# U pass of a PEER block: activations' high and low halves side by side, one 512-column matmul in place of two of 256 columns

## The chip, the cores and the metric

One core of one Trainium2 chip. The metric is the device time of the kernel in microseconds (us); lower is better. A profile of one execution lies beside the times.

## The reference, cut to what matters

The kernel computes one hybrid block: a mixer (pooling heads and latent attention), and then a feed-forward part, PEER, a retrieval over 16,384 single-neuron experts. Only the latter is touched:

```
def peer_ffn(h, w_q, sub_keys, expert_u, expert_v):       # h: 256 tokens x 2048
    q = (hf @ w_q).reshape(t, 8, 2, 128)
    sc = einsum('thpd,hpnd->thpn', q, sub_keys)           # scores against 2 x 128 sub-keys
    sv, si = top_k(sc, 16)                                # per head and half
    cand = sv[:, :, 0, :, None] + sv[:, :, 1, None, :]    # 16 x 16 pairs
    best, pos = top_k(cand, 16)
    eidx = ...                                            # 8 x 16 experts a token
    gate = softmax(best)
    u = take(expert_u, eidx);  a = einsum('ted,td->te', u, x)
    act = gelu(a, approximate=False) * gate
    vv = take(expert_v, eidx); out = einsum('te,ted->td', act, vv)
```

Everything is float32.

## The kernel before

The kernel gathers nothing: it multiplies all 16,384 experts with all 256 tokens, and puts the gates of the experts that were not picked to zero. So after the mixer there are three stages:

- The **U pass**: `acts = gelu(expert_u @ h2)`, in 128 tiles of 128 experts. A tile's 128x2048 floats of `expert_u` come as two halves of 128x1024 (512 KB each, four DMAs), into one of four buffers `raw`.
- The **gates** ("hot" stage): one-hot products spread the picked gates over the experts, and DVE multiplies them into `acts`.
- The **V pass**: `acts @ expert_v`, again in 128 tiles.

To keep float32's precision at the speed of the rounded type `fp32r`, each operand x is split in a high part xH (x rounded to `fp32r`) and a low part xL = x - xH, and each product is three: H·H, H·L and L·H. In the U pass the expert half is the stationary operand (`eH`, `eL`, three ring slots each), and the activations `h2H` and `h2L` (16 k-tiles of 256 tokens) are the moving one. The three products of a k-tile are `split3` (lines 603 to 605), all into one accumulation of 256 columns in one of the three PSUM banks `ps[:, 0..2, 0:256]`.

A half tile j goes through the engines so:

1. DMA (queue of SP) into `raw[j % 4]`, after the low part of half j-4 was made.
2. DVE transposes it in place in 32x32 blocks (`u_round`, line 1593).
3. ACT rounds it to `eH` (`u_high`, line 1151), once PE is through with half j-3, whose ring slot it takes (`u_used`).
4. The low part: DVE makes `eL` for even halves (`u_low`, line 1584), POOL for odd ones (`low_round`, line 504). Both subtract `eH` from `raw`.
5. PE: 8 k-tiles of 3 matmuls (`u_tile`).
6. After a tile's second half ACT applies Gelu straight from PSUM to `acts` (`gelu`, line 1164), and increments `a_out`. PE starts a tile once `a_out` says that the tile three before it has left its bank.

Each engine runs its own instructions in the order of the program; the kernel is written by hand in rounds of 6 tiles (12 halves), 21 rounds and 2 tiles more, of which most are hardware loops. DVE has other work in the U pass, placed between the transposes: for 16 groups of 6 halves (rounds 0 to 7) the top-16 of the sub-key scores, for 8 groups (rounds 8 to 11) the top-16 of the pairs, and in rounds 12 to 15 twelve steps that turn the picks into expert indices (`sub_keys`). One group's picks are six steps, one behind each half's transpose (and behind `u_low` where j is odd):

```
step 0: two copies cand<-sc  (pairs: two additions cand<-s16,s16)
step 1: two MAX8              step 2: two FIND_INDEX8, two MATCH_REPLACE8
step 3: two MAX8              step 4: two FIND_INDEX8
step 5: four small copies (CAST i16f/posu<-picked_at, COPY s/best<-picked)
```

Step 0 stands behind the first half of a group, step 5 behind the sixth.

## Time and profile before

| | before |
|---|---|
| device time, median of 3 runs | 2263.73 us (2262.08 to 2267.1) |
| profiled execution, span from first to last instruction | 2260.1 us |
| PE / DVE / ACT / POOL busy | 89% / 69% / 41% / 30% |
| U pass on PE, first to last matmul | 679.98 to 1421.28 us |
| V pass on PE | from about 1550 us to near the end |

The page names no device time of its own for the profiled execution; its span lies 3.6 us under the median of the runs, which also take in what stands ahead of the first and behind the last instruction. Times within a span are microseconds from its start. PE's busy time counts pipelined matmuls from their start to their modelled end; how fast it goes is read from the distance between starts. A line of the profile is that of the kernel before.

### The profile page before, as it was taken

Reading aid. Unit: us, or ns where it says so; the run is one execution under the profiler, and the core shown is the slowest. Engines: PE = TensorE matmul, PEld = TensorE weight load, DVE = VectorE, ACT = ScalarE, POOL = GpSimd, SP = SyncE. Lnnn points to the kernel's source line nnn. Section 1 sums busy time; section 2 is a strip of 40 time slices with the busy share of each in tenths; the row PEclk is TensorE's granted clock in tenths of the full one; section 3 lists DMA queues with packets and bytes.
Section 4 is the critical chain, followed back from the end, with each engine's and each line's share of the span. In section 5 each row is a group of like instructions: output and inputs, shape, how many; then the busy total and the mean of one; then the engine's idle time right before and its main releaser. Section 6 shows DMA issues by size and latency. Waiting matters only on the chain.

```text
span 2260.1 us, 38640 instructions
## 1 busy us (share of the span) xinstructions
PE 2012.3 (89%) x12649; PEld 1780.7 (79%) x12649; DVE 1555.6 (69%) x2214; ACT 918.7 (41%) x1399; POOL 687.8 (30%) x462
## 2 busy tenths in 40 slices
PE   1797978856889999999999999668999999999996
PEld 1675646745779999999999999657888888888885
DVE  5778679537449999999997666896555555555554
ACT  1133223335334444444444444564444444444443
POOL 0056015745644444444444444781000000000000
PEclk9988956888989999999999999999999999999998
DMA  9975586772956666666666666006565556555563
GB/s 355 359 276 218 201 325 236 274 192 76 274 155 179 185 182 180 182 181 184 176 176 183 182 182 170 28 0 218 192 193 193 193 191 193 193 194 192 193 194 121
DMA packets 264038, 439.13 MB, mean 194 GB/s; under 512 B 22242, under 2 KB 156688, under 8 KB 262192
## 3 DMA queue, kind: packets, MB, share of 16 engines
q1 hardware_dynamic: 262368, 427.89, 61.7%
q0 software_dynamic: 1600, 10.51, 1.2%
q8 instruction: 33, 0.54, 0.1%
q14 instruction: 21, 0.17, 0.0%
q10 hardware_dynamic: 16, 0.02, 0.0%
HBM read 434.12 MB, written 4.21 MB: 194 GB/s over the span
## 4 chain that ended last, share of the span: by engine, by line
PE 66%; DVE 19%; DMA 8%; issue 2%; ACT 2%; DVEq 1%; SPq 1%; POOL 0%; ACTq 0%; POOLq 0%
PE ps L926 10%; PE ps L923 10%; PE ps L924 10%; PE ps L603 10%; PE ps L605 10%; PE ps L604 10%; DMA ring<-in_ada_w_dram 7%; DVE acc L1272 6%; DVE acc_b L1272 6%; DVE hotB L1635 2%; PE ps L598 2%; DMA ring<-in_peer_wq_dram 1%; DVE acc_b L1269 1%; DVEq L1635 1%; PE ps L576 1%
## 5 line engine op out<-in xcount | busy, mean ns | idle before, releaser
L603 PE MATMUL ps<-h2H,eH 128*128 128x256 f32 x2048 | 580.1, 283 | 3.6 <-DVE eL L1584 2.3
L604 PE MATMUL ps<-h2L,eH 128*128 128x256 f32 x2048 | 579.6, 283 | 0.0
L605 PE MATMUL ps<-h2H,eL 128*128 128x256 f32 x2048 | 579.5, 283 | 0.0
L1666 DVE TENSOR_TENSOR eL<-raw,eH 128x1024 fp32r<-128x1024 f32 x256 | 313.5, 1225 | 338.3 <-ACT eH L1222 338.3
L504 POOL TENSOR_TENSOR eL<-raw,eH 128x1024 fp32r<-128x1024 f32 x128 | 311.0, 2430 | 451.7 <-ACT eH L1151 451.7
L1222 ACT CAST eH<-raw 128x1024 fp32r<-128x1024 f32 x256 | 269.9, 1055 | 385.4 <-PE ps L926 376.0
L923 PE MATMUL ps<-eH,aH 128*128 128x512 f32 x1024 | 399.0, 390 | 3.6 <-DVE eL L1666 3.6
L924 PE MATMUL ps<-eL,aH 128*128 128x512 f32 x1024 | 398.8, 389 | 0.0
L603 PEld LDWEIGHTS ps<-h2H,eH 128*128 128x128 f32 x2048 | 393.1, 192 | 4.6 <-POOL eL L504 1.7
L604 PEld LDWEIGHTS ps<-h2L,eH 128*128 128x128 f32 x2048 | 393.2, 192 | 0.0
L605 PEld LDWEIGHTS ps<-h2H,eL 128*128 128x128 f32 x2048 | 393.2, 192 | 0.0
L1593 DVE STREAM_TRANSPOSE raw<-raw 128x1024 f32<-128x1024 f32 x256 | 317.5, 1243 | 87.6 <-DMA raw<-in_peer_u_dram 79.3
L1151 ACT CAST eH<-raw 128x1024 fp32r<-128x1024 f32 x256 | 267.3, 1045 | 196.7 <-PE ps L605 158.7
L926 PE MATMUL ps<-eH,aL 128*128 128x512 f32 x1024 | 316.0, 390 | 0.0
L923 PEld LDWEIGHTS ps<-eH,aH 128*128 128x128 f32 x1024 | 192.6, 188 | 43.7 <-issue 3.7
L924 PEld LDWEIGHTS ps<-eL,aH 128*128 128x128 f32 x1024 | 192.6, 188 | 40.1
L926 PEld LDWEIGHTS ps<-eH,aL 128*128 128x128 f32 x1024 | 192.6, 188 | 40.0
L347 POOL TENSOR_TENSOR result<-x,scaled 128x2048 f32<-128x2048 f32 x1 | 4.5, 4471 | 712.1 <-DVEq L1687 712.1
L1584 DVE TENSOR_TENSOR eL<-raw,eH 128x1024 fp32r<-128x1024 f32 x128 | 154.1, 1204 | 32.9 <-ACT eH L1151 32.6
L1272 DVE SCALAR_TENSOR_TENSOR acc_b<-ring,c_act,acc_b 128x512 f32<-128x512 f32 x168 | 169.4, 1008 | 0.0
L1272 DVE SCALAR_TENSOR_TENSOR acc<-ring,c_act,acc 128x512 f32<-128x512 f32 x168 | 167.4, 996 | 0.6 <-DVE s_sb L1430 0.2
L1164 ACT ACTIVATE acts<-ps 128x256 f32 (+1 forms) x128 | 49.2, 385 | 224.6 <-PE ps L605 224.6
(267 smaller groups left out, 2717.6 us busy)
## 6 DMA issues: line engine op xcount, KB each, us to landing
raw<-in_peer_u_dram SPq DMA_DIRECT2D x1024, 128.0 KB, 2.9
raw<-in_peer_v_dram SPq DMA_DIRECT2D x256, 512.0 KB, 4.7
ring<-in_ada_w_dram SPq DMA_DIRECT2D x24, 4096.0 KB, 14.6
ring<-in_w_out_dram SPq DMA_DIRECT2D x4, 4096.0 KB, 20.0
ring<-in_peer_wq_dram SPq DMA_DIRECT2D x16, 1024.0 KB, 21.8
ring<-in_w_in_dram SPq DMA_DIRECT2D x3, 4096.0 KB, 13.5
ring<-in_w_uq_dram SPq DMA_DIRECT2D x1, 3072.0 KB, 18.1
ring<-in_w_in_dram SPq DMA_DIRECT2D x1, 2560.0 KB, 13.8
```

What stands on the lines that cost most here:

```text
L504: pool.tensor_tensor(by_k(eL[:, j % RING, :]), turned(raw[:, j % RAW, :]), by_k(eH[:, j % RING, :].bitcast(F32)), ALU.subtract).then_inc(u ...
L603: pe.matmul(o, lh, rh, start=start, stop=False, skip_group_check=True)
L604: pe.matmul(o, lh, rl, start=False, stop=False, skip_group_check=True)
L605: return pe.matmul(o, ll, rh, start=False, stop=stop, skip_group_check=True)
L923: pe.matmul(o[n], lh, vh[n], start=start, stop=False, skip_group_check=True)
L924: pe.matmul(o[n], lh, vl[n], start=False, stop=False, skip_group_check=True)
L926: mm = pe.matmul(o[n], ll, vh[n], start=False, stop=stop, skip_group_check=True)
L1151: act.copy(by_k(eH[:, j % RING, :]), turned(raw[:, j % RAW, :])).then_inc(u_hi, 1)
L1222: act.copy(eH[:, slot, :], raw[:, slot, :]).then_inc(v_hi, 1)
L1272: ins = dve.scalar_tensor_tensor(s_, w[:, k, :], c_act[:, k:k + 1], init[:, n % 2, :] if k == 0 else s_, ALU.mult, ALU.add)
L1593: dve.transpose(raw[:, j % RAW, :], raw[:, j % RAW, :]).then_inc(u_tr, 1)
L1666: dve.tensor_tensor(eL[:, slot, :], raw[:, slot, :], eH[:, slot, :].bitcast(F32), ALU.subtract).then_inc(v_lo, 1)
```

## The change

`h2H` and `h2L` are no longer two tensors one behind the other but one, `h2`, of [k-tile, 2, 256]: a k-tile's high and low halves lie side by side. So the two matmuls with the stationary `eH` become one with 512 columns into a full PSUM bank: `eH·h2H` lands in columns 0 to 255, `eH·h2L` in columns 256 to 511. `eL·h2H` is added to the first half as before. Before the Gelu the two halves of the bank must be added: ACT copies the second half to `asum` in SBUF (`cross_half`), DVE adds the first one from PSUM (`halves_sum`), and ACT's Gelu reads `asum`. The Gelu comes one tile later in ACT's program than before, the copy stands behind even `u_high`s, the addition behind the odd halves' `u_low`; PE's wait for a free bank is now for the addition (`a_sum`). `asum` has two buffers of 256 columns, in place of a row buffer that is no longer in use by then.

```
-    h2H = at("h2H", M, [KT, T], F32R)
-    h2L = at("h2L", M + 4096, [KT, T], F32R)
+    h2 = at("h2", M, [KT, 2, T], F32R)
+    h2H, h2L = h2[:, :, 0, :], h2[:, :, 1, :]
+    asum = at("asum", S + 688, [2, T])
...
             def u_tile(r, i, first):
                 if not first:
-                    pe.wait_ge(a_out, tile - 2)
+                    pe.wait_ge(a_sum, tile - 2)
...
-                        mm = split3(ps[:, bank, 0:T], eH[:, slot, k * P:(k + 1) * P], eL[:, slot, k * P:(k + 1) * P],
-                                    h2H[:, kk, :], h2L[:, kk, :], kk == 0, kk == KT - 1)
+                        pe.matmul(ps[:, bank, :], eH[:, slot, k * P:(k + 1) * P], h2[:, kk].rearrange("p a t -> p (a t)"),
+                                  start=kk == 0, stop=False, skip_group_check=True)
+                        mm = pe.matmul(ps[:, bank, 0:T], eL[:, slot, k * P:(k + 1) * P], h2H[:, kk, :],
+                                       start=False, stop=kk == KT - 1, skip_group_check=True)
...
-            def gelu(tile, bank):
+            def cross_half(tile, bank, half, first=False):
                 act.wait_ge(u_used, tile * 2 + 2)
-                act.activation(acts[:, bass.ds(tile, 1), :], ps[:, bank, 0:T], ACT.Gelu).then_inc(a_out, 1)
+                if first:
+                    act.wait_ge(row_stored, 128)
+                else:
+                    act.wait_ge(a_out, tile - 1)
+                act.copy(asum[:, half, :], ps[:, bank, T:2 * T]).then_inc(a_cross, 1)
+
+            def gelu(tile, half):
+                act.wait_ge(a_sum, tile + 1)
+                act.activation(acts[:, bass.ds(tile, 1), :], asum[:, half, :], ACT.Gelu).then_inc(a_out, 1)
...
-                    if j % 2 == 1 and not (first and j == 1):
-                        gelu(r * ROUND + (j // 2 - 1), (j // 2 - 1) % 3)
+                    if j % 2 == 0 and not (first and j < 4):
+                        cross_half(r * ROUND + (j // 2 - 2), (j // 2 - 2) % 3, j // 2 % 2, first and j < 8)
+                    elif j % 2 and not (first and j < 7):
+                        gelu(r * ROUND + (j // 2 - 3), (j // 2 + 1) % 2)
...
+            def halves_sum(tile, bank, half):
+                dve.wait_ge(a_cross, tile + 1)
+                dve.tensor_tensor(asum[:, half, :], ps[:, bank, 0:T], asum[:, half, :], ALU.add).then_inc(a_sum, 1)
...
                     if j % 2:
                         u_low(r, j - 1, first and j - 1 < RING)
+                        if not (first and j < 5):
+                            halves_sum(r * ROUND + (j // 2 - 2), (j // 2 - 2) % 3, j // 2 % 2)
```

What this makes of DVE's program, at the end of a group of picks of the sub-key stage and the start of the next (the loop of rounds 1 to 7; L1593 or L1613 is the transpose, L1584 or L1600 is `u_low`). Before:

```order
L1593 STREAM_TRANSPOSE raw<-raw 128x1024
L1581 REGISTER_ALU
L1583 REGISTER_ALU
L1584 TENSOR_TENSOR eL<-raw,eH 128x1024
L1539 ISA
L1539 COPY i16f<-picked_at 128x16
L1540 REGISTER_ALU
L1540 COPY s_66<-picked 128x16
```

And now:

```order
L1613 STREAM_TRANSPOSE raw<-raw 128x1024
L1597 REGISTER_ALU
L1599 REGISTER_ALU
L1600 TENSOR_TENSOR eL<-raw,eH 128x1024
L1604 REGISTER_ALU
L1605 TENSOR_TENSOR asum<-ps,asum 128x256
L1555 ISA
L1555 COPY i16f<-picked_at 128x16
```

The addition (L1605) has come between `u_low` and step 5's copies, and stands so at every odd half.

PE's program at the start of the U pass (ahead of it the transposes of the sub-keys and their scores). Before:

```order
L842 MATMUL ps<-cst,ring_49 128x128 x16
L854 MATMUL ps<-keyT,qT 128x128 x32
L603 MATMUL ps<-h2H,eH 128x256
L604 MATMUL ps<-h2L,eH 128x256
L605 MATMUL ps<-h2H,eL 128x256
```

And now (`h_144` is the tensor h2):

```order
L842 MATMUL ps<-cst,ring_49 128x128 x16
L854 MATMUL ps<-keyT,qT 128x128 x32
L867 MATMUL ps<-h_144,eH 128x512
L869 MATMUL ps<-h_144,eL 128x256
L867 MATMUL ps<-h_144,eH 128x512
```

Two matmuls and two weight loads a k-tile where there were three of each, with 768 columns as before.

## Rows read from the trace of the kernel before

**Rows 1.** The page: busy time by engine, and the chain that ended last.

```profile
PE 2012.3 (89%) x12649; PEld 1780.7 (79%) x12649; DVE 1555.6 (69%) x2214; ACT 918.7 (41%) x1399; POOL 687.8 (30%) x462
...
PE 66%; DVE 19%; DMA 8%; issue 2%; ACT 2%; DVEq 1%; SPq 1%; POOL 0%; ACTq 0%; POOLq 0%
```

**Rows 2.** Timeline, PE in the U pass: start, duration, engine, line, operation.

```profile
1200.07 0.28 PE L603 MATMUL ps<-h2H,eH 128*128 128x256 f32 x1
1200.19 0.28 PE L604 MATMUL ps<-h2L,eH 128*128 128x256 f32 x1
...
1421.28 0.28 PE L605 MATMUL ps<-h2H,eL 128*128 128x256 f32 x1
```

**Rows 3.** Windows, V pass: stretch, length, busy PE, PEld, DVE, ACT, POOL, PEclk, DMA, GB/s.

```profile
2000.00:2200.00 200.00, 200.00 (x885) 165.58 (x884) 102.49 (x110) 88.61 (x111) 0.00 (x0) 1.00 0.59 193
```

**Rows 4.** Windows, four stretches of the U pass.

```profile
692.87:948.60 255.73, 255.73 (x2134) 255.73 (x2133) 234.97 (x465) 106.28 (x134) 105.38 (x44) 1.00 0.68 183
948.60:1087.20 138.60, 138.60 (x1158) 138.60 (x1157) 135.94 (x248) 57.67 (x73) 57.55 (x24) 1.00 0.64 182
1087.20:1202.94 115.74, 113.28 (x940) 112.67 (x939) 107.27 (x79) 55.66 (x66) 52.16 (x20) 1.00 0.66 175
1216.00:1416.00 200.00, 200.00 (x1669) 200.00 (x1668) 123.87 (x103) 82.76 (x106) 83.35 (x35) 1.00 0.67 176
```

**Rows 5.** Timeline, first group of sub-key picks, step 5 and the next transpose.

```profile
687.95 1.25 DVE L1593 STREAM_TRANSPOSE raw<-raw 128x1024 f32<-128x1024 f32 x1 [0.45 <-DVE picked_at L1537]
689.12 1.18 DVE L1584 TENSOR_TENSOR eL<-raw,eH 128x1024 fp32r<-128x1024 f32 x1
689.23 1.05 ACT L1151 CAST eH<-raw 128x1024 fp32r<-128x1024 f32 x1 [1.16 <-DVE raw L1593]
690.22 0.17 DVE L1539 CAST i16f<-picked_at 128x16 f32<-128x16 uint32 x1
690.36 2.44 POOL L504 TENSOR_TENSOR eL<-raw,eH 128x1024 fp32r<-128x1024 f32 x1 [2.60 <-ACT eH L1151]
690.45 2.38 DVE L1540 COPY s<-picked 128x16 f32<-128x16 f32 x1
692.87 1.25 DVE L1593 STREAM_TRANSPOSE raw<-raw 128x1024 f32<-128x1024 f32 x1
```

**Rows 6.** Timeline, end of the second group of sub-key picks.

```profile
704.04 1.25 DVE L1593 STREAM_TRANSPOSE raw<-raw 128x1024 f32<-128x1024 f32 x1
706.42 1.05 ACT L1151 CAST eH<-raw 128x1024 fp32r<-128x1024 f32 x1 [1.61 <-PE ps L605]
706.54 0.17 DVE L1540 COPY s<-picked 128x16 f32<-128x16 f32 x1
707.54 2.40 POOL L504 TENSOR_TENSOR eL<-raw,eH 128x1024 fp32r<-128x1024 f32 x1 [3.25 <-ACT eH L1151]
```

**Rows 7.** Timeline, one group of pair picks: first, last half.

```profile
1000.92 1.25 DVE L1593 STREAM_TRANSPOSE raw<-raw 128x1024 f32<-128x1024 f32 x1
1001.38 2.39 POOL L504 TENSOR_TENSOR eL<-raw,eH 128x1024 fp32r<-128x1024 f32 x1 [3.36 <-ACT eH L1151]
1002.09 2.31 DVE L1525 TENSOR_TENSOR cand<-s 128x256 f32 x2
1015.51 1.25 DVE L1593 STREAM_TRANSPOSE raw<-raw 128x1024 f32<-128x1024 f32 x1
1018.01 0.16 DVE L1540 COPY best<-picked 128x16 f32 x1
1018.31 1.25 DVE L1593 STREAM_TRANSPOSE raw<-raw 128x1024 f32<-128x1024 f32 x1
```

**Rows 8.** Timeline, gates stage: a DVE product with one operand in PSUM, and POOL.

```profile
1442.12 0.62 POOL L518 TENSOR_TENSOR hotP<-cst,slotT 128x256 f32<-128x256 f32 x1 [0.75 <-PE ps L901]
1442.18 0.67 DVE L1641 TENSOR_TENSOR acts<-acts,ps 128x512 f32 x1
```

**Rows 9.** Timeline, ACT's last Gelu.

```profile
1421.60 0.38 ACT L1164 ACTIVATE acts<-ps 128x256 f32<-128x256 f32 x1 [5.37 <-PE ps L605]
```

More of the change, by code:

```diff
@@ L260, in hybrid_block @@
         u_tr, u_hi, u_lo, u_lo_pool, u_used = sem("u_tr"), sem("u_hi"), sem("u_lo"), sem("u_lo_pool"), sem("u_used")
-        a_out = sem("a_out")
+        a_cross, a_sum, a_out = sem("a_cross"), sem("a_sum"), sem("a_out")
         hot_pool, hot_act, hot_abs, hot_diff = sem("hot_pool"), sem("hot_act"), sem("hot_abs"), sem("hot_diff")
@@ L1188, in _ @@
             u_round(ROUNDS, TILES % ROUND)
+            cross_half(TILES - 2, (TILES - 2) % 3, 0)
+            gelu(TILES - 3, 1)
+            cross_half(TILES - 1, (TILES - 1) % 3, 1)
+            gelu(TILES - 2, 0)
             gelu(TILES - 1, 1)
@@ L1627, in _ @@
             u_round(ROUNDS, TILES % ROUND)
+            halves_sum(TILES - 2, (TILES - 2) % 3, 0)
+            halves_sum(TILES - 1, (TILES - 1) % 3, 1)
             def hots(g, half, first):
```

## The prediction

> **What bounds the kernel now.** I read the page's busy times and its chain first [rows 1]: PE is busy for 89% and carries 66% of the chain, DVE 19%. That is an average, so next the stretches of the stage that is changed. In the U pass PE is 100% busy in the two stretches of picks and after them, at granted clock 1.00 [rows 4]; the timeline shows matmuls of 256 columns starting 0.12 us apart without a gap [rows 2]. Counted over the last stretch it is 200 us / 1669 = 0.1198 us [rows 4]. So a half tile takes 24 x 0.12 = 2.88 us on PE, a group of six halves 17.28, and PE sets the pace. But look at DVE in the same rows: 234.97 of 255.73 us (92%) while it picks sub-keys, 135.94 of 138.60 (98%) while it picks pairs, 107.27 of 115.74 (93%) with `sub_keys`, and only 62% after that. In three of the four stretches the second engine is full behind the first, and the change takes time from PE and gives work to DVE.
>
> **PE's part.** The V pass has matmuls of 512 columns, each with its own weight load: 200 us / 885 = 0.226 us apart, at the same clock [rows 3]. So columns cost 0.106 us per 256, and each pair of load and matmul about 0.013 us on top. A k-tile of the U pass goes from 3 x 0.12 = 0.36 us to 0.226 + 0.12 = 0.346, a tile from 5.76 to 5.536, a half to 2.768, a group to 16.6 us. Over 128 x 16 k-tiles that is 27.6 to 29 us, if PE stays the bound. The bounds of this price are nothing (a matmul of 512 costing two of 256) and this.
>
> The Trainium skill ("TensorE: Matmul & The Clock Gate", Back-to-back issue gap) gives N/2.4 + 2.5 ns for the distance of two matmuls at full clock: 109 and 216 ns, by which a k-tile would save 2.5 ns and the whole pass 5 us. The rows have 120 and 226, so I go by the rows.
>
> **DVE's part.** One addition a tile, 256 columns, one operand in PSUM. The nearest row is DVE's product of 512 columns with PSUM, 0.67 us [rows 8]; a DVE row of 1024 columns from SBUF is 1.18 [rows 5], next start 1.10 after its own, so about 1.04 ns a column. That leaves 0.67 - 0.27 = 0.40 for the addition, of which 0.34 keeps the next one waiting (a duration less 0.07 of overlap). Bounds: 0.27 (columns alone) and 0.45.
>
> Whether it can get stuck: in rows 8 POOL began a subtraction with two SBUF operands at 1442.12, and DVE's product began 0.06 later and still took 0.67, so an addition of this kind doesn't wait for POOL. The opposite kind is in rows 5 and 7. POOL's `eL` ran from 690.36 to 692.80; DVE's small copy of 690.45, otherwise 0.17 us, ended at 692.83. And the first of two pair additions, begun at 1002.09, waited for the end of POOL at 1003.77, after which both took 0.63. Copies in SBUF and additions with both operands there stand still until POOL is through.
>
> The Trainium skill says the same ("SBUF — State Buffer", Who interferes with whom): a DVE instruction with at most one SBUF input outside the two-port modes doesn't contend with GpSimd, two SBUF inputs or a two-port copy do. By that rule the new addition is safe and the old copies aren't.
>
> What matters is therefore not the 0.34 us alone but where step 5's copies now fall. Take T as the start of a group's sixth transpose. If ACT waits for nothing else, its rounding starts 1.28 later, and POOL's `eL` runs from T + 2.41 to T + 4.85 (687.95, 689.23, 690.36 and 2.44 long) [rows 5]. The four copies start at T + 2.27 now: three slipped in ahead of POOL there, and the fourth was caught. In the second group DVE had caught up, ACT waited for PE until 706.42, POOL began only at T + 3.50, and all four copies slipped by [rows 6]. So before, DVE loses its time to POOL in step 0 instead (1.68 us in rows 7), and still keeps up. With the addition the copies come to T + 2.60, behind POOL's start: all four stand until T + 4.85, and the next transpose starts at T + 5.16 rather than T + 2.6.
>
> **DVE's cycle after the change.** Sub-key group without any lock: 692.87 to the end of the last copy 706.71, 13.84 us [rows 5, 6]. Take out the last 2.6, put in 5.16, and two more additions of 0.34 (the third is inside the lock): 17.08. Step 0 then meets no POOL. Pair group: 1000.92 to 1018.31 is 17.39, less 1.68 of lock and 0.14 of waiting = 15.57 [rows 7]; less 2.66, plus 5.16, plus 0.68 = 18.75. Both are over PE's 16.6, so DVE becomes the bound, ACT waits for DVE and not for PE, and the assumption that POOL starts at T + 2.41 holds itself up: DVE never gets the lead that let the copies escape. It is a tight thing at the entry: in the second group T would come near 704.97, its transpose end at 706.2, and PE would be ready for ACT at 705.4, 0.8 us earlier.
>
> Sum, in PE's time, against the profiled 2260.1:
> - Sub-key stage, some 15 groups of 17.08 in place of 17.28: -3.
> - Pair stage, 8 groups of 18.75 in place of 17.28: +11.7.
> - The 38 halves with `sub_keys`. DVE's 115.7 us hold 8.5 of idleness [rows 4]; most of it goes (-6.5), 19 additions come (+6.4, of which some 1.3 inside locks), and the four big products behind odd halves, which begin at 2.27 after their transpose and now at 2.60, fall behind POOL's start as the copies do; I put that at 3 us over those locks that are there already: 117.3. PE took 38 x 2.88 = 109.4 for these halves, and 4 of gaps: the whole pass lasted from 679.98 to 1421.4 [rows 2], 4.1 more than 128 x 5.76, and of the four stretches this is the only one in which PE wasn't busy throughout [rows 4]. 117.3 in place of 113.4: +4.
> - The 74 halves left, DVE at 62%: 74 x 0.113 = -8.4.
> - The end: ACT's Gelu started right behind the last matmul [rows 2, 9]. Now a copy of 0.38, the addition 0.40 and two handovers of 0.1 stand ahead of it: +1.
>
> Together +5.3: span 2265.4. The median of the runs lies 3.6 above the profile's span, so 2269. Elsewhere nothing moves: ACT's copies (0.38 a tile) fall in an engine that is 42% busy in these stretches [rows 4], and PE's wait for `a_sum` is for an addition that stands in DVE's program ahead of the `eL` which the same tile needs anyway.
>
> **The rivals.**
> 1. *DVE keeps its lead (faster).* If at the entry, or after any pause of PE, POOL's `eL` starts past T + 2.9, the copies escape and the lock falls in step 0, at least 1.2 us. Then a sub-key group needs 13.84 + 1.02 + 1.2 = 16.1 and runs at PE's 16.6 (-10.9 over 16), the pair group at 15.57 + 1.02 + 1.2 = 17.8 (+4), `sub_keys` at +2, the rest as above: -12, so 2252. For it: the state of before is of this kind. Against: it takes 0.8 us that DVE doesn't have at the start. 0.16. It decides from the point where ACT waits for PE at the sixth half.
> 2. *The saving shows in full*, DVE's additions hidden: -27.6 + 1, 2237. Against it, 98% in rows 4. 0.05.
> 3. *The addition is dearer*, 0.45 us a piece or a wait for ACT's copy in DVE's queue, behind which everything stands: 0.1 more for two additions in each of 24 groups and half as many after, some +6: 2275. 0.12.
> 4. *A matmul of 512 saves nothing*: the stages bound by DVE stay, the last loses its -8.4: 2277. For it there is no row, against it rows 3. 0.06. The formula of the Trainium skill cited above ("TensorE: Matmul & The Clock Gate", Back-to-back issue gap) would come out here but for 2.5 ns a k-tile.
> 5. *The lock is half as long in the pair stage* (POOL held up by DVE's own `eL` now and then): +1, 2265. 0.09.
> 6. *The addition waits for POOL after all*: 2 us in most odd halves, +50 and more. Rows 8 speak against it. 0.02.
>
> The forecast itself has 0.50, with a range of its own from 2264 to 2274.
>
> **How the numbers follow.** A measurement of this kernel tells about 0.2% (4.5 us) from no change, so "same" is 2259.2 to 2268.3. The forecast's middle is just above that edge: 0.3 of its 0.5 is slower and 0.2 same. Slower: 0.3 + 0.12 + 0.06 + 0.02 = 0.50. Same: 0.2 + 0.09 + 0.02 (of rival 1) = 0.31. Faster: 0.14 + 0.05 = 0.19. The range takes in rivals 1, 3, 4 and 5 and leaves out 2 and 6: 2250 to 2279.
>
> **What would show it.** In the changed kernel's trace: matmuls 0.226 and 0.12 us apart in the last stretch, which then runs at 5.54 us a tile; PE idle in small gaps, some 0.5 us a group in the sub-key stage and 2 in the pair stage, waiting for `eL`; ACT's roundings there released by DVE's transposes, not by PE; the copies of step 5 at over 2 us and those of step 0 short; DVE near 100%. Wrong would be: step 0 still carrying the lock with ACT released by PE (rival 1), additions over 0.5 us (3 or 6), or spacing that doesn't add to 0.346 (4).

## The result, and the profile after

| | before | after |
|---|---|---|
| device time, median | 2263.38 us (2262.08 to 2267.1, 4 runs) | 2274.93 us (2273.46 to 2278.31, 4 runs) |
| span of the profiled execution | 2260.1 us | 2272.2 us |
| U pass, first to last matmul | 741.3 us | 747.6 us |

The ratio is 1.005, interval 1.0036 to 1.0064: the kernel became 11.5 us slower, where 5.3 were forecast; its median lies 5.9 over the forecast's 2269. One execution of the kernel before, beside the second set of experiments, took 2896 us at a granted clock of 0.65 and is left out of every comparison. The page of the changed kernel, busy time by engine, the chain that ended last, and two groups that the change touches ([rows 1] are the first two lines before; the last line here is the group of ACT's roundings in the kernel before):

```profile
PE 2002.0 (88%) x10601; PEld 1668.7 (73%) x10601; DVE 1598.0 (70%) x2342; ACT 955.6 (42%) x1527; POOL 686.0 (30%) x462
...
PE 50%; DVE 28%; DMA 10%; issue 6%; ACT 3%; SPq 2%; DVEq 1%; POOL 0%; ACTq 0%; POOLq 0%
...
L867 PE MATMUL ps<-h,eH 128*128 128x512 f32 x2048 | 723.1, 397 | 21.5 <-DVE eL L1600 21.2
...
L1153 ACT CAST eH<-raw 128x1024 fp32r<-128x1024 f32 x256 | 269.1, 1051 | 386.5 <-DVE raw L1613 279.2
...
L1151 ACT CAST eH<-raw 128x1024 fp32r<-128x1024 f32 x256 | 267.3, 1045 | 196.7 <-PE ps L605 158.7
```

PE has 2048 matmuls fewer, as it should, and in the chain PE gave way to DVE: 50% for 66%, 28% for 19%. PE's first matmul of a half now waits 21 us in all for DVE's low part, and most of ACT's idle time before its roundings, 279.2 of 386.5 us, ends with a transpose of DVE, where before 158.7 of 196.7 ended with PE. The stage by stage view is the windows of the U pass, cut at the same transposes as [rows 4] (length, busy time of PE, PEld, DVE, ACT and POOL, granted clock, DMA share, GB/s); the last one is 200 us out of the stretch behind them:

```profile
696.88:955.40 258.52, 256.42 (x1446) 220.46 (x1445) 252.11 (x510) 122.28 (x181) 107.96 (x45) 1.00 0.68 183
955.40:1106.28 150.88, 139.62 (x771) 117.53 (x770) 148.23 (x273) 64.43 (x96) 57.47 (x24) 1.00 0.60 167
1106.28:1221.45 115.17, 108.25 (x607) 92.34 (x606) 110.53 (x99) 59.99 (x84) 49.21 (x19) 1.00 0.65 173
1230.00:1430.00 200.00, 200.00 (x1155) 176.11 (x1154) 135.77 (x141) 95.50 (x144) 86.00 (x36) 1.00 0.72 183
```

Against [rows 4]: the sub-key stretch 258.5 us for 255.7, the pairs 150.9 for 138.6, the stretch with `sub_keys` 115.2 for 115.7. The granted clock is 1.00 in all. In the first two PE is no longer full (it has 0.14 and 1.4 us of idleness a group, where 0.5 and 2 were forecast) and DVE is, at 98% both times. From there to the last matmul it is 210.0 us for 218.3; counted over the last row, 1155 matmuls in 200 us are 0.346 us for each pair of them. So the whole account of the U pass is +0.1 before the first of these marks, +2.8, +12.3, -0.6, -8.3: +6.3.

In what follows a small copy or an addition is called caught, or in a lock, when it lasts until POOL's subtraction is through instead of its usual few tenths of a microsecond. The timeline of DVE, POOL and ACT in the second group of sub-key picks, around the sixth transpose (start, duration, engine, line, operation, and in brackets the idle time before and what ended it), which answers to [rows 5] and [rows 6]:

```profile
708.71 1.25 DVE L1613 STREAM_TRANSPOSE raw<-raw 128x1024 f32<-128x1024 f32 x1
709.99 1.05 ACT L1153 CAST eH<-raw 128x1024 fp32r<-128x1024 f32 x1 [0.46 <-DVE raw L1613]
710.99 0.41 DVE L1605 TENSOR_TENSOR asum<-ps,asum 128x256 f32<-128x256 f32 x1
711.12 2.40 POOL L504 TENSOR_TENSOR eL<-raw,eH 128x1024 fp32r<-128x1024 f32 x1 [2.49 <-ACT eH L1153]
711.32 2.24 DVE L1555 CAST i16f<-picked_at 128x16 f32<-128x16 uint32 x1
...
713.93 1.25 DVE L1613 STREAM_TRANSPOSE raw<-raw 128x1024 f32<-128x1024 f32 x1
```

Read it from T = 708.71. ACT is released by the transpose, not by PE as in [rows 6]. POOL starts at T + 2.41, the addition ends in time for the first small copy at T + 2.61, and that copy takes 2.24 us until POOL is through. The next transpose stands at T + 5.22. Step 0 behind it is quick: its two copies take 0.32. From the third group on one time is different: POOL starts later behind ACT's rounding.

```profile
727.07 1.25 DVE L1613 STREAM_TRANSPOSE raw<-raw 128x1024 f32<-128x1024 f32 x1 [0.95 <-DMA raw<-in_peer_u_dram]
728.35 1.05 ACT L1153 CAST eH<-raw 128x1024 fp32r<-128x1024 f32 x1 [1.39 <-DVE raw L1613]
729.56 2.39 POOL L504 TENSOR_TENSOR eL<-raw,eH 128x1024 fp32r<-128x1024 f32 x1 [3.81 <-ACT eH L1153]
```

Now T = 727.07, and POOL starts at T + 2.49. The first two groups are the round that is written out, the others run in hardware loops: in all 13 traces here POOL's subtraction starts 0.077 us behind the end of ACT's rounding in the six odd halves of the first round and the two of the last, and 0.157 in the loop between them. The next transpose stands 5.17 to 5.29 behind T there, but for the last group of pairs.

The groups of DVE's instructions over the picks, before and after, show where the lock has gone (line, operation, count, busy us, mean ns). Before, from 710 to 1080:

```profile
L1528 DVE COPY cand<-sc 128x128 f32 x28 | 32.7, 1207 | 0.0
L1525 DVE TENSOR_TENSOR cand<-s 128x256 f32 x16 | 18.6, 1199 | 0.0
L1539 DVE CAST i16f<-picked_at 128x16 uint32 x28 | 4.5, 168 | 0.0
```

After, from 710 to 1100:

```profile
L1555 DVE CAST i16f<-picked_at 128x16 uint32 (+1 forms) x30 | 36.8, 1232 | 0.0
L1605 DVE TENSOR_TENSOR asum<-ps,asum 128x256 f32<-128x256 f32 x66 | 27.3, 414 | 0.0
...
L1541 DVE TENSOR_TENSOR cand<-s 128x256 f32 x16 | 5.8, 399 | 0.0
L1544 DVE COPY cand<-sc 128x128 f32 x28 | 4.5, 201 | 0.0
```

Step 0's copies and additions fell from 1207 and 1199 ns to 201 and 399, and step 5's first copies rose from 168 to over 1200. They come in pairs of which one is caught and one is short, so the mean hides a piece of 2.2 or 2.3 us in each. The addition itself costs 27.3 us in 66 pieces and was never caught: over the pass it is 410 ns at least and 425 at most.

### The profile page after: what moved, and what is told of

Read it like the earlier page. It is cut to its first block, busy times and chain, and to the rows that moved or that the text cites. A ratio compares the mean times of both kernels' runs of the same rounds, so it can differ in the third digit from the quotient of the medians.

```text
span 2272.2 us, 35008 instructions
## 1 busy us (share of the span) xinstructions
PE 2002.0 (88%) x10601; PEld 1668.7 (73%) x10601; DVE 1598.0 (70%) x2342; ACT 955.6 (42%) x1527; POOL 686.0 (30%) x462
## 4 chain that ended last, share of the span: by engine, by line
PE 50%; DVE 28%; DMA 10%; issue 6%; ACT 3%; SPq 2%; DVEq 1%; POOL 0%; ACTq 0%; POOLq 0%
PE ps L925 10%; PE ps L926 10%; PE ps L928 10%; PE ps L867 10%; DVE acc L1288 6%; DMA ring<-in_ada_w_dram 6%; DVE acc_b L1288 5%; PE ps L869 5%; DVE raw L1613 2%; DVE eL L1600 2%; DVE hotB L1659 2%; PE ps L598 2%; DMA raw<-in_peer_u_dram 2%; ACT eH L1153 2%; DMA init<-in_ada_b_dram 1%
## 5 line engine op out<-in xcount | busy, mean ns | idle before, releaser
L867 PE MATMUL ps<-h,eH 128*128 128x512 f32 x2048 | 723.1, 397 | 21.5 <-DVE eL L1600 21.2
L869 PE MATMUL ps<-h,eL 128*128 128x256 f32 x2048 | 573.2, 280 | 0.0
L867 PEld LDWEIGHTS ps<-h,eH 128*128 128x128 f32 x2048 | 384.0, 188 | 122.8 <-DVE eL L1600 31.5
L1153 ACT CAST eH<-raw 128x1024 fp32r<-128x1024 f32 x256 | 269.1, 1051 | 386.5 <-DVE raw L1613 279.2
L869 PEld LDWEIGHTS ps<-h,eL 128*128 128x128 f32 x2048 | 386.5, 189 | 0.0
L1613 DVE STREAM_TRANSPOSE raw<-raw 128x1024 f32<-128x1024 f32 x256 | 316.8, 1241 | 78.7 <-DMA raw<-in_peer_u_dram 69.9
L1600 DVE TENSOR_TENSOR eL<-raw,eH 128x1024 fp32r<-128x1024 f32 x128 | 152.5, 1192 | 11.5 <-ACT eH L1153 11.1
L1288 DVE SCALAR_TENSOR_TENSOR acc<-ring,c_act,init 128x512 f32<-128x512 f32 x24 | 27.1, 1131 | 129.3 <-DMA ring<-in_ada_w_dram 111.9
L474 POOL TENSOR_TENSOR ring_low<-ring,win_high 128x512 fp32r<-128x512 f32 (+1 forms) x48 | 67.2, 1436 | 141.4 <-ACT win_high L991 141.2
L474 POOL TENSOR_TENSOR ring_low<-ring,wq_high 128x512 fp32r<-128x512 f32 x64 | 93.4, 1490 | 49.7 <-ACT wq_high L991 48.7
```

The costliest lines, as they stand in the source:

```text
L867: pe.matmul(ps[:, bank, :], eH[:, slot, k * P:(k + 1) * P], h2[:, kk].rearrange("p a t -> p (a t)"), start=kk == 0, stop=False, skip_group ...
L869: mm = pe.matmul(ps[:, bank, 0:T], eL[:, slot, k * P:(k + 1) * P], h2H[:, kk, :], start=False, stop=kk == KT - 1, skip_group_check=True)
L1153: act.copy(by_k(eH[:, j % RING, :]), turned(raw[:, j % RAW, :])).then_inc(u_hi, 1)
L1288: ins = dve.scalar_tensor_tensor(s_, w[:, k, :], c_act[:, k:k + 1], init[:, n % 2, :] if k == 0 else s_, ALU.mult, ALU.add)
L1600: dve.tensor_tensor(by_k(eL[:, j % RING, :]), turned(raw[:, j % RAW, :]), by_k(eH[:, j % RING, :].bitcast(F32)), ALU.subtract).then_inc(u_ ...
L1613: dve.transpose(raw[:, j % RAW, :], raw[:, j % RAW, :]).then_inc(u_tr, 1)
```

## The experiments

Two theories stood against each other at the start. The first: the additions fill DVE, and what decides is which of DVE's SBUF copies meet POOL's subtraction. The second: PE saves little by itself, and the additions or the waits cost what they cost wherever they stand. Medians are set beside runs of the kernel before on the same chip (2262.3, 2262.2 and 2262.4 us in the three sets). A "group" is six halves, timed from transpose to transpose in the one execution that was profiled. One number is the mean of a stage's groups, of which single ones lie some 0.6 us to either side. The first group of a stage is left out, and so are single ones in which DVE also waited for data: in the changed kernel the one of 18.31. First the table, then the edits.

| run | median, us | ratio and interval | sub-key group | pair group | last stretch, a group |
|---|---|---|---|---|---|
| after | 2274.9 | 1.005 (1.0036 to 1.0064) | 17.05 to 17.22 | 18.83 to 18.95 | 16.64 |
| copies early | 2252.05 | 0.9958 (0.9942 to 0.9975) | 16.64 | 17.31 | 16.96 |
| copies early, kernel before | 2262.96 | 1.0 (0.999 to 1.0009) | 17.28 | 17.28 | 17.28 |
| no addition | 2242.96 | 0.9915 (0.9898 to 0.9931) | 16.96 | 16.96 | 16.96 |
| addition twice | 2291.66 | 1.013 (1.0113 to 1.0147) | 17.75 to 17.88 | 19.49 to 19.61 | 16.64 |
| both moved | 2248.57 | 0.9935 (0.9918 to 0.9953) | 16.9 | 16.9 | 16.64 |
| addition behind the copies | 2254.72 | 0.9963 (0.9948 to 0.9978) | 15.6 to 16.96 | 17.32 | 16.96 |
| POOL adds | 2273.03 | 1.0053 (1.0033 to 1.0073) | 16.96 | 17.4 to 17.7 | 16.64 |
| addition within SBUF | 2279.96 | 1.0077 (1.0055 to 1.0099) | 17.18 to 17.37 | 18.9 to 19.0 | 16.64 |
| kernel before with additions | 2277.6 | 1.0062 (1.0042 to 1.0083) | 17.10 to 17.27, then 15.07 to 17.39 | 18.84 to 18.95 | 17.28 |
| spread | 2244.52 | 0.992 (0.9905 to 0.9935) | 16.64 | 16.64 | 16.64 |
| turned order | 2241.23 | 0.9899 (0.9884 to 0.9914) | 16.7 | 16.7 | 16.7 |

**Step 5's copies early.** The four copies stand directly behind the sixth transpose, ahead of `u_low`, when POOL can't have started:

```
                     dve.transpose(raw[:, j % RAW, :], raw[:, j % RAW, :]).then_inc(u_tr, 1)
+                    if pairs is not None and j % 6 == 5:
+                        pick_step(r * 2 + j // 6, 5, pairs)
                     if j % 2:
                         u_low(r, j - 1, first and j - 1 < RING)
...
-                    if pairs is not None and not (first and j == 0):
+                    if pairs is not None and not (first and j == 0) and j % 6 < 5:
                         pick_step(r * 2 + j // 6, j % 6, pairs)
```

> Changed kernel with the four copies of step 5 moved ahead of the even half's eL subtraction (they start 1.2 us after the sixth transpose's start, before POOL can begin at 2.4). Lock theory (DVE is the bound and loses 2.2 us a group behind POOL at step 5): a sub-key group falls from 17.16 us to PE's 16.6, a pair group from 18.9 to about 17.6 (what is left is some 1 us of lock at step 0); in all -8 and -10, so about 2256 us, 7 below the kernel before. Work theory (the additions' own 0.34 us are what costs, the lock only moves to step 0): a pair group stays over 18.5, the time within 3 us of 2275. Handover theory (ACT's copy and the longer chain to Gelu delay PE): no change, 2275.

2252.05 us, 10.3 below the kernel before where the changed one is 11.5 above it, so some 22 us better, with every addition still in place. The groups of DVE, 710 to 1080, of this run:

```profile
L1544 DVE COPY cand<-sc 128x128 f32 x26 | 27.6, 1100 | 0.0
...
L1541 DVE TENSOR_TENSOR cand<-s 128x256 f32 x16 | 12.8, 838 | 0.0
...
L1555 DVE CAST i16f<-picked_at 128x16 uint32 x28 | 4.0, 150 | 0.0
```

The lock is back in step 0, where it was before the change, and step 5 is short again. A lock there is cheaper, since step 0 comes when POOL has already run for a part of its 2.4 us, as in [rows 7]: against the 0.20 and 0.40 that these pieces take in the changed kernel it costs 1.8 us in a sub-key group, where PE sets the pace again, and 0.9 in a pair group, where step 5's cost 2.1. So some two thirds of what the additions seemed to cost (31 us, below) hung on the place of four copies of 0.17 us.

**The same edit in the kernel before.**

> The kernel before with the same move of step 5's copies, a control. Lock theory: PE is the bound there and DVE has no gain to pass on, 2263 within 3 us. Rival (the move helps by itself, since DVE lies on the path at the start and in the stretch with the index steps): 5 us or more below 2263.

2262.96 us, no change, groups 17.28: there PE sets the pace, and the place of the copies is worth nothing. The gain of the first run comes only where DVE is the bound.

**No addition.** ACT copies the first half of the bank to `asum`, and nothing is added; `eH·h2L` is left out of the result:

```
-                    pe.wait_ge(a_sum, tile - 2)
+                    pe.wait_ge(a_cross, tile - 2)
...
-                act.copy(asum[:, half, :], ps[:, bank, T:2 * T]).then_inc(a_cross, 1)
+                act.copy(asum[:, half, :], ps[:, bank, 0:T]).then_inc(a_cross, 1)
...
-                act.wait_ge(a_sum, tile + 1)
+                act.wait_ge(a_cross, tile + 1)
...
-                            halves_sum(r * ROUND + (j // 2 - 2), (j // 2 - 2) % 3, j // 2 % 2)
```

> Changed kernel without DVE's addition: ACT's copy takes the first half of the bank instead of the second, and Gelu reads that, so the product eH x h2L is left out of the result; PE and ACT do all that they do in the changed kernel. Lock and work theory alike: DVE is back at 13.8 us a sub-key group and keeps its lead, PE sets 16.6 us there and about 17 in the pair stage, the last stretch 16.6; together about 2240 (2234 to 2246). Handover theory (ACT's copy in the chain, or matmuls of 512 in this mix, cost the time): 2265 to 2275.

2242.96 us: the matmuls and ACT's copies alone are worth 19.4 us against the kernel before, and the additions as the change places them cost 31 (19.4 and 11.5). That ACT's copy or the longer way to the Gelu should cost the time is out. Its profiled execution was the longest of the four, 2251.58 us; the last section comes back to it.

**The addition twice** (the first of the two into columns of the bank that nobody reads any more):

```
                 dve.wait_ge(a_cross, tile + 1)
+                dve.tensor_tensor(ps[:, bank, T:2 * T], ps[:, bank, 0:T], asum[:, half, :], ALU.add)
                 dve.tensor_tensor(asum[:, half, :], ps[:, bank, 0:T], asum[:, half, :], ALU.add).then_inc(a_sum, 1)
```

> Changed kernel with each addition done twice (the first result goes to the bank's other half and is not used). If DVE is the bound: 0.34 us for each of the two additions of a group that stand outside the lock, 24 groups, +16, and some +5 in the stretch with the index steps, nothing after it: about 2296. If DVE were not the bound (handover theory): under +5, 2280.

2291.66 us. DVE's timeline at the sixth half of this kernel:

```profile
710.97 0.42 DVE L1605 TENSOR_TENSOR ps<-ps,asum 128x256 f32<-128x256 f32 x1
711.31 0.41 DVE L1606 TENSOR_TENSOR asum<-ps,asum 128x256 f32<-128x256 f32 x1
711.64 1.90 DVE L1555 CAST i16f<-picked_at 128x16 f32<-128x16 uint32 x1
...
713.91 1.25 DVE L1614 STREAM_TRANSPOSE raw<-raw 128x1024 f32<-128x1024 f32 x1
```

The second addition starts 0.34 us after the first; the caught copy is shorter by as much (1.90 for 2.24), and the next transpose stands at 713.91 as it stood at 713.93. An addition inside the lock costs nothing, the two others of a group 0.34 each: the groups grew by some 0.65. That is the price that the prediction gave it.

**Both moved.** As the first, and step 0 too goes ahead of POOL's start: behind the second transpose of a group instead of the first, ahead of `u_low`:

```
...
+                    if pairs is not None and j % 6 == 1 and not (first and j == 1):
+                        pick_step(r * 2 + j // 6, 0, pairs)
                     if j % 2:
                         u_low(r, j - 1, first and j - 1 < RING)
+                        if pairs is not None and j % 6 == 1 and not (first and j == 1):
+                            pick_wait(r * 2 + j // 6, 1)
...
```

> Changed kernel with step 5's copies ahead of the even half's eL, as in the run before, and step 0's two operations moved behind the next half's transpose, ahead of its eL, where POOL has ended. Lock theory: no copy or pick addition waits for POOL any more; a pair group falls from 17.3 us to 16.65 (15.57 + 1.02 of additions, as much as PE's 16.6), a sub-key group stays at PE's pace; 8 x 0.65 = 5 us less than with the copies alone, about 2247. Rival (17.3 us a pair group is plain DVE work and not a lock at step 0): within 2 us of 2252.

2248.57 us, 13.6 below the kernel before where the copies alone gave 10.3. DVE's groups, 710 to 1080:

```profile
L1613 DVE STREAM_TRANSPOSE raw<-raw 128x1024 f32<-128x1024 f32 x131 | 162.9, 1244 | 37.0 <-DMA raw<-in_peer_u_dram 32.4
...
L1541 DVE TENSOR_TENSOR cand<-s 128x256 f32 x16 | 5.7, 399 | 0.0
```

Step 0 is free of POOL as step 5 is, and DVE has 37 us to spare ahead of its transposes where it now waits for data; PE is the bound in the pair stage again.

**The addition behind the copies**, in the sixth half alone. The prediction would have it that the copies then start at T + 2.27, where three slip by and the fourth is caught, as in [rows 5]:

```
-                        if not (first and j < 5):
+                        if not (first and j < 5) and not (pairs is not None and j % 6 == 5):
...
                         pick_step(r * 2 + j // 6, j % 6, pairs)
+                    if pairs is not None and j % 6 == 5:
+                        halves_sum(r * ROUND + (j // 2 - 2), (j // 2 - 2) % 3, j // 2 % 2)
```

> Changed kernel with the addition of the sixth half behind step 5's copies instead of ahead of them, nothing else moved. Place theory (what hurts is that the addition pushes the copies behind POOL's start): three copies slip by, all is well, below 2263. Lock theory in full (with DVE as the bound POOL starts 2.41 us after the transpose and the fourth copy is caught at 2.5, as in the first group of the kernel before; one caught copy costs as much as four): 17.1 us a sub-key group, 18.9 a pair group, 2275 to 2278.

2254.72 us, 20 below the 2275 to 2278 that were expected. The timeline in the second group and in a pair group:

```profile
710.12 2.44 POOL L504 TENSOR_TENSOR eL<-raw,eH 128x1024 fp32r<-128x1024 f32 x1 [2.50 <-ACT eH L1153]
710.21 2.38 DVE L1556 COPY s<-picked 128x16 f32<-128x16 f32 x1
...
999.26 2.45 POOL L504 TENSOR_TENSOR eL<-raw,eH 128x1024 fp32r<-128x1024 f32 x1 [3.13 <-ACT eH L1153]
999.27 0.17 DVE L1556 COPY best<-picked 128x16 f32 x1
```

The fourth copy was caught in the first two groups, 2.38 us. From the third on ACT's rounding still begins at T + 1.28 where DVE releases it, but POOL starts at T + 2.49 in place of T + 2.41, with the later handover of the loop, and the copy (999.27, with POOL in front at 999.26) gets through in 0.17. The groups shrink to 15.6 to 16.5 us while DVE catches up, and then ACT waits for PE in the sub-key stage. The escape doesn't need that: in the pair stage ACT is released by DVE's transpose again, at T + 1.28, and the copies get through in all eight groups. What the expectation had wrong was POOL's start, read from [rows 5], the first group, outside the loop. The same few tenths of DVE's work, on the other side of four short copies, are worth 20 us.

**POOL adds.** ACT copies the whole bank of 512 columns, POOL adds its halves behind its own `eL`, with the copies early; PE's wait for a bank is then for ACT's copy:

```
+            def halves_sum(tile):
+                pool.wait_ge(a_cross, tile + 1)
+                pool.tensor_tensor(asum[:, 0, :], asum[:, 0, :], asum[:, 1, :], ALU.add).then_inc(a_sum, 1)
...
-                    act.wait_ge(a_out, tile - 1)
-                act.copy(asum[:, half, :], ps[:, bank, T:2 * T]).then_inc(a_cross, 1)
+                    act.wait_ge(a_out, tile)
+                act.copy(asum[:].rearrange("p a t -> p (a t)"), ps[:, bank, :]).then_inc(a_cross, 1)
```

> Copies of step 5 early as in the first run; ACT copies the whole bank (512 columns) to SBUF and POOL adds the halves there (behind its own eL) in place of DVE; Gelu and copy follow one another in ACT. DVE has 13.84 and 15.57 us of its own a group and at most 2 us of lock at step 0 behind a POOL that is now busy 0.6 us longer: 16.6 a sub-key group, 17.2 a pair group, less waiting in the stretch with the index steps; about 2246 (2240 to 2252). If POOL's addition delays its next eL or DVE's eL: 2255 and more.

2273.03 us, a miss by 27. The sub-key groups run at 16.96 as hoped, but with `sub_keys` a group takes 19.2 to 21.5 us. POOL's additions from 720 to 940, then from 1110 to 1220, and one of the latter with what DVE did:

```profile
L511 POOL TENSOR_TENSOR asum<-asum 128x256 f32<-128x256 f32 x39 | 29.0, 743 | 0.0
...
L511 POOL TENSOR_TENSOR asum<-asum 128x256 f32<-128x256 f32 x16 | 25.6, 1600 | 0.0
...
1140.10 2.10 DVE L1608 TENSOR_TENSOR eL<-raw,eH 128x1024 fp32r<-128x1024 f32 x1
1141.08 1.72 POOL L511 TENSOR_TENSOR asum<-asum 128x256 f32<-128x256 f32 x1
```

The same addition takes POOL 743 ns in one stage and 1600 in the other. Fourteen of the 16 in the second began while DVE's `u_low`, a subtraction with both operands in SBUF, was running, and took 1.71 to 1.74 us; the two others took 0.73. So POOL is held by DVE as DVE is by POOL, and the low part that PE waits for comes late: 12.0 us of PE's idleness in this stretch end with POOL's `eL`.

**The addition within SBUF.** ACT copies the whole bank as above, DVE adds the two SBUF halves at the place of the change:

```
-                dve.tensor_tensor(asum[:, half, :], ps[:, bank, 0:T], asum[:, half, :], ALU.add).then_inc(a_sum, 1)
+                dve.tensor_tensor(asum[:, 0, :], asum[:, 0, :], asum[:, 1, :], ALU.add).then_inc(a_sum, 1)
```

> Changed kernel, with ACT copying the whole bank (512 columns) to SBUF and DVE adding the two halves there: the same DVE work, but two operands in SBUF. If such an addition shares a port with POOL: it starts some 0.14 us ahead of POOL's eL, which then begins 0.25 later, and with it the end of the lock: 17.3 us a sub-key group, 19.1 a pair group, some +5, 2280; where POOL is first, the addition takes over 2 us. If it shares nothing: 17.16 and 18.9, 2275, and no addition over 0.45 us.

2279.96 us, where I had put it, and the timeline shows the hold that was under test, though shorter than expected. One of the first groups, and a sixth half in the loop:

```profile
705.71 0.41 DVE L1605 TENSOR_TENSOR asum<-asum 128x256 f32<-128x256 f32 x1
705.85 2.54 POOL L504 TENSOR_TENSOR eL<-raw,eH 128x1024 fp32r<-128x1024 f32 x1 [2.19 <-ACT eH L1153]
...
728.57 0.42 DVE L1605 TENSOR_TENSOR asum<-asum 128x256 f32<-128x256 f32 x1
728.78 2.44 POOL L504 TENSOR_TENSOR eL<-raw,eH 128x1024 fp32r<-128x1024 f32 x1 [3.19 <-ACT eH L1153]
728.90 2.36 DVE L1555 CAST i16f<-picked_at 128x16 uint32 x1
```

The addition begins up to 0.2 us before POOL's subtraction and is through undisturbed, the copy behind it is caught. But now POOL is held: in the two stages of picks its subtraction takes 2.53 to 2.54 us where 0.28 us of the addition were left at its start, 2.44 to 2.48 where some 0.2 were left (35 times), and 2.38 to 2.41 where less was left or nothing. In the changed kernel, whose addition has one operand in PSUM, the same overlaps leave it at 2.38 to 2.42. The other direction was met once: the addition at 1431.19, which began when 0.19 us of POOL's subtraction were left, took 0.47 us, the longest of the 128. The groups are 0.07 to 0.08 us longer, which isn't all of the 6 us between the two kernels, and the rest wasn't looked for.

**The kernel before, with additions.** The three matmuls of 256 columns stay. ACT's copies and DVE's additional instructions stand as in the change; as there is no second half to add, DVE takes the maximum of the bank and its copy, which leaves the values as they are:

```
...
+                act.copy(asum[:, half, :], ps[:, bank, 0:T]).then_inc(a_cross, 1)
...
+                dve.tensor_tensor(asum[:, half, :], ps[:, bank, 0:T], asum[:, half, :], ALU.max).then_inc(a_sum, 1)
```

> Only the DVE and ACT half of the change, without PE's: three matmuls of 256 columns as before, all into the first half of the bank; ACT copies that half to asum, DVE takes the maximum of PSUM and asum (equal numbers, so the result stays) with the same shapes as the addition, Gelu from asum. If DVE's cycle is what costs: sub-key groups 17.2 to 17.3 (DVE's 17.16 just below PE's 17.28), pair groups 18.9 in place of 17.28, +13, the stretch with the index steps +2 or 3, the rest at 17.28: about 2278 (2274 to 2282), slower than the changed kernel by what PE gains there in the last stretch. If the matmuls of 512 columns had a part in the loss: about 2265.

2277.6 us. Windows of the pair stage and of the stretch behind the picks, and what ACT waited for from 968 to 1100 (us in all, times, longest):

```profile
968.00:1100.00 132.00, 125.15 (x1018) 122.51 (x1017) 129.61 (x239) 56.34 (x84) 50.13 (x22) 1.00 0.58 166
1240.00:1420.00 180.00, 180.00 (x1503) 180.00 (x1502) 123.39 (x126) 84.77 (x128) 74.60 (x32) 1.00 0.71 182
```

```profile
ACT eH L1151 <- DVE raw L1611: 75.9, 42, 4.0
```

DVE's side alone, with ACT released by its transposes, makes the pair groups 18.9 us long, the same as in the changed kernel, whatever PE's matmuls cost. With DVE loaded so, the wide matmul is worth some 4 us (15.2 above the kernel before without it, 11.5 with it); without the additions it was worth 19.4. The last stretch, where DVE has room, keeps 17.28 a group here for 16.64. In the sub-key stage DVE's 17.2 us are just below PE's 17.28: in eleven groups a copy of step 5 is caught, from the twelfth on ACT waits for PE long enough for all to get through, until the pair stage.

**Spread.** Both moved, and the twelve steps of `sub_keys` no longer behind halves 4, 7, 10 to 37 but further apart:

```
-                    at_ = j + 2 * ROUND * i - 4
-                    if at_ >= 0 and at_ % 3 == 0 and at_ // 3 < 12:
-                        sub_keys(at_ // 3)
+                    places = (4, 8, 11, 14, 18, 21, 24, 28, 31, 34, 38, 41)
+                    if j + 2 * ROUND * i in places:
+                        sub_keys(places.index(j + 2 * ROUND * i))
```

> Both picks' steps moved as in e5, and the twelve index steps at halves 4, 8, 11, 14, 18, 21, ... in place of every third: the big products with two SBUF operands behind even halves alone, where POOL is at most 1 us from its end, the sums (which take no second port) behind odd ones. Lock theory: the 38 to 42 halves of this stretch go from 117 us to near PE's pace (48 halves in 136 rather than 142), 2242 (2239 to 2246). Rival (the stretch is bound by DVE's plain work, 2.3 us a step): 2247 to 2250.

2244.52 us, as expected (2239 to 2246); the 38 halves with `sub_keys` take 109.7 us where both moved, the kernel that it is made from, needed 116.9 and the changed one 115.2.

**Turned order.** The last, and in every second k-tile the matmul with `eL` stands first, so that the sequence is 512, 256, 256, 512:

```
...
+                        if kk % 2:
+                            low()
+                            mm = high()
+                        else:
+                            high()
+                            mm = low()
```

> e10 with the order of the two matmuls turned in every second k-tile, so that two of 512 and two of 256 columns follow one another. In the traces so far PE goes at one of two paces when nothing holds it up, 0.3467 or 0.3533 us a k-tile, in the same program. If the alternation of 512 and 256 columns is what makes the slower pace possible: 0.346 throughout, some 10 us below e10, 2232. If not: the same two paces and e10's time within 3 us.

2241.23 us, all four executions within 2240.34 to 2242.51, where the five of the kernel it is made from lay between 2241.7 and 2248.56. The 2232 that were expected if the alternation alone made the slower pace did not come, and the 3.3 us under that kernel lie within the spread of its executions. It beats both kernels: 21 us or 1% under the one before, some 33 under the changed one. What the traces show of the order is told at the end.

## Why the prediction was right or wrong

The direction was called, with the mechanism; the size was half of what came: +5.3 forecast, +11.5 measured, +12.0 between the two profiled spans. By its steps:

- *PE's part.* 0.346 us a k-tile was forecast, and the last stretch has 0.346. The bound "a matmul of 512 columns saves nothing" (rival 4) is out: the saving is 13 ns a k-tile (17.28 less 16.64 us over 48). The formula of the Trainium skill ("TensorE: Matmul & The Clock Gate", Back-to-back issue gap), which that section gives for isolated matmuls, made it 2.5 ns, and the trace doesn't agree. One thing was not seen, that this pace has a second value, with half the saving (below).
- *DVE's part.* The addition was put at 0.40 with 0.34 on the path: 0.41 and 0.34. It was never held (425 ns at most), nor did DVE wait ahead of it in the picks, so rivals 3 and 6 are out. In the changed kernel only two of the 128 began while POOL was at work, but with the addition twice 90 did, and none of them took over 0.44 us. The rule of the Trainium skill ("SBUF — State Buffer", Who interferes with whom) that an instruction of DVE with at most one SBUF input, outside its two-port modes, doesn't contend with GpSimd agrees with these.
- *The lock moves from step 0 to step 5.* Forecast were copies at T + 2.60 and the next transpose at T + 5.16; measured 2.61 and 5.22, and in the loop 2.61 and 5.17 to 5.29, as POOL starts 0.08 us later there than in [rows 5]. The copies-early run and the one with the addition behind them show that this, more than DVE's load as such, is what costs: they give 22 and some 20 us back with all additions in place, of the 31 that the additions cost. The unchanged result of the same edit in the kernel before shows that it matters only where DVE is the bound.
- *DVE keeps its lead (rival 1)* did not come in the changed kernel. It did in the kernel before with additions, from the twelfth group on, where PE's 17.28 us a group leave DVE time to catch up.
- *Rivals 2 and 5* are out too: DVE is at 98% in both stages of picks, so the saving can't show in full, and the caught copy of a pair group takes 2.3 us, as long as that of a sub-key group.
- *The sum, sub-key stage*: "some 15 groups of 17.08 in place of 17.28: -3". In the time of DVE's transposes this is 256.2 forecast, and 258.5 came: fourteen groups of 17.05 to 17.22 and one of 18.31. This term was mis-sized by 2.3 us, more than any other: some 1.1 is POOL's later start in the loop, 0.08 us in each of fourteen groups, and 1.2 the one group, in which DVE waits 0.42 and 0.95 us for the data of two halves.
- *Pair stage*: 150.0 forecast, 150.9 measured, 18.9 a group for 18.75, of which 0.08 again is POOL's start in the loop.
- *The 38 halves with `sub_keys`*: 117.3 forecast, 115.2 measured. The allowance of 3 us for more products behind POOL's start and 6.4 for the additions was too dear: DVE's busy time grew by 3.3 us [rows 4] where the step implies 8; its idle time fell by 3.8 and not 6.5.
- *The halves left*: -8.4 forecast, -8.3 measured. *The end*: +1 forecast; from the last matmul to the first of the gates it is 3.46 us for 2.92, +0.5.
- The U pass came out at +6.3 for +4.3. As summed, against PE's time, the sub-key term was -3 and the `sub_keys` term +4; between the windows of the two kernels they came out as +2.8 and -0.6. One reason is that the sum took 259.2 and 113.4 us as the time of before, where the transposes took 255.7 and 115.7. That the two misses, of 5.8 and 4.6, went opposite ways and the U pass as a whole missed by only 2 is luck.
- That leaves, between the two profiled executions, 3.9 us ahead of the first matmul of the U pass (683.87 for 679.98) and 1.3 in the gates and the V pass, which the sum took as fixed. In the other kernels of this study that first matmul stands anywhere from 678.2 to 684.3, so 3.9 us is within what one execution differs from the next. But the medians are as far apart as the profiled executions, and no run tells whether the changed kernel starts its U pass late more often. Of the 1.3, 1.0 is the V pass, 698.8 us from first to last matmul for 697.8, and this goes with the change: it takes 697.8 in all three kernels with three matmuls a k-tile and 698.3 to 699.0 in all ten with the wide one, in one profiled execution each, though the edit doesn't touch its program. The cause is open. Some 5 of the 11.5 us stay unexplained.

So the steps on the mechanism held, and the error is in the sum: 2 us in the U pass, and what lies outside it.

## What to carry to other kernels

When a change takes time from the engine that sets the pace and gives work to the second one, look at each stage's windows for the second engine's share, not at the total: here 92 to 98% in three stretches decided it. Then look at where that engine's SBUF copies fall against the other engine's long two-operand work, to a tenth of a microsecond; short instructions that can go ahead of its start should, and moving them cost nothing here. With that done the change that had lost 11.5 us won 14, and with two more edits of the order alone 21. An offset that is read outside a loop need not hold within it: here POOL started 0.08 us later in the loop, and that decided which copies were caught.

## What the runs showed that was not expected

**A copy of 16 elements costs 0.17 or 2.4 us, by some hundredths of a microsecond between its start and POOL's.** In the run with the addition behind the copies, one began 0.09 us after POOL's instruction and took 2.38 us; another began 0.01 us after it by the trace and took 0.17. Over all 13 traces 110 such copies began while POOL's subtraction ran: the 15 that began at most 0.017 us behind its start took 0.17 us, the 95 that began 0.033 us or more behind it took 1.9 to 2.4. A schedule near that edge can change sides within one execution, as two runs show: the one with the addition behind the copies, where POOL starts later in the loop, and the kernel before with additions, where DVE's groups are a little shorter than PE's.

**PE's pace with alternating widths has two values.** These are windows of the same two stretches where nothing held PE, a few hundred microseconds apart, in one execution each. Copies early:

```profile
720.00:940.00 220.00, 220.00 (x1272) 193.97 (x1271) 216.42 (x446) 106.67 (x159) 95.92 (x40) 1.00 0.69 190
...
1220.00:1400.00 180.00, 180.00 (x1023) 156.13 (x1022) 123.86 (x127) 86.05 (x130) 75.12 (x33) 1.00 0.69 179
```

Both moved:

```profile
720.00:940.00 220.00, 220.00 (x1248) 190.82 (x1247) 190.21 (x443) 104.32 (x157) 92.92 (x40) 1.00 0.73 186
...
1220.00:1400.00 180.00, 180.00 (x1042) 158.84 (x1041) 123.83 (x128) 88.08 (x132) 77.33 (x33) 1.00 0.72 183
```

All four have PE full at granted clock 1.00, and in each kernel one stretch runs at 0.346 us a k-tile (1272 matmuls in 220 us, 1042 in 180) and the other at 0.352 (1248 and 1023), in the opposite order. By the groups of six halves, 48 k-tiles, it is 16.64 and 16.96 us, 0.347 and 0.353 each; over the whole pass that would be 14 us. The timeline shows it in the matmuls themselves. Copies early, at the slower pace:

```profile
1299.60 0.40 PE L867 MATMUL ps<-h,eH 128*128 128x512 f32 x1
1299.84 0.28 PE L869 MATMUL ps<-h,eL 128*128 128x256 f32 x1
1299.96 0.40 PE L867 MATMUL ps<-h,eH 128*128 128x512 f32 x1
```

Spread, at the faster one:

```profile
1299.87 0.40 PE L867 MATMUL ps<-h,eH 128*128 128x512 f32 x1
1300.10 0.28 PE L869 MATMUL ps<-h,eL 128*128 128x256 f32 x1
1300.22 0.39 PE L867 MATMUL ps<-h,eH 128*128 128x512 f32 x1
```

0.24 and 0.12 from start to start in the one, 0.23 and 0.12 in the other. The run without additions was profiled at 2251.58 us with all groups at 16.96, and its three other executions took 2242.5 to 2243.0; that fits a pace that is chosen anew in each execution, but those others have no trace. With the order turned both stretches have one pace between the two, near 0.348, and the times lie within 2.2 us; one trace isn't proof that it is always so. Part of what spread gained on both moved, in its profiled execution, is this pace: 16.6 us a group in the picks for 16.9. What picks the pace wasn't found. The kernel before, with all matmuls at 256 columns, showed 0.12 us throughout.
